# Five of eight prompt tiles gather their experts, three are multiplied with all experts in table order

## The chip, the cores and the metric

One core of one Trainium2 chip runs the whole layer as one program. The metric is device time in microseconds, the median of several runs. Everything is computed in float32.

## What is computed

One layer of an encoder over two groups of tokens, 1024 of the prompt and 256 of the sample: a mixer (windowed and dense attention, two gates, three projections), then PEER, a retrieval of experts, and an RMSNorm. The change is in PEER for the prompt:

```python
def one_chunk(xc):                      # 128 tokens of the normed input
    qry = einsum('cd,dq->cq', xc, w_query).reshape(128, 8, 2, 128)
    sc = einsum('chpd,hpnd->chpn', qry, sub_keys)         # 2 x 128 scores a head
    s_top, i_top = top_k(sc, 16)
    cand = s_top[:, :, 0, :, None] + s_top[:, :, 1, None, :]
    best_s, pos = top_k(cand.reshape(128, 8, 256), 16)
    idx = i_top[0] * 128 + i_top[1]     # taken at pos: 16 of 16384 experts a head
    g = softmax(best_s)
    u, v = expert_u[idx], expert_v[idx] # rows of 1024
    act = gelu(einsum('chkd,cd->chk', u, xc))
    return einsum('chk,chkd->cd', g * act, v)
```

A token takes 8 x 16 = 128 experts. A row of U and its row of V stand beside each other in one table `experts`, 8 KB together; the table has 16384 rows, 134 MB.

## The kernel before

The program runs its stages one after the other, with barriers between: projection, attention and merge of the sample, a stage that picks the sample's experts, then the same for the prompt with the sample's experts gathered beside them, and last `phase_experts` for the prompt's eight tiles of 128 tokens. The change replaces this last stage.

All orders are written out by hand. Each engine has its own list of instructions and waits on counters (semaphores) of the others. A tile has 128 slots (one expert for each of 128 tokens). For every slot GpSimd (POOL) issues one indirect DMA that gathers 128 rows of 8 KB into one of the RING = 8 places of `ring`, 1.05 MB (L1685). Two slots are a step, 64 steps a tile (STEPS, PAIR). In a step g, `tile` of each engine does this:

- DVE multiplies the U half of two slots with the tile's h and sums (L1930, "dot"), and multiplies the gelu of the step before with the gates (L1924, `wgt`).
- ACT takes the gelu of two dots (L1756) and writes, for the step before, two diagonal matrices from the weights (L1762, `diag`).
- PE multiplies the diagonals with the V halves and adds to `acc` in PSUM; each step is 16 products on 32x32 parts of the array, 32 records in the trace (L2032), then counts `used`.
- POOL waits for `used` of four steps back (BACK) before it gathers into the same place.

Between these steps stands the choice for the next tile, head by head: the query products (L1993), the scores (L2002), and on DVE `choose` in three parts (the top 16 of two lists of 128, then of their 256 sums, then the index: L1805 to L1859). Only head 0 of the first tile is chosen before the first gather. At the end of a tile `acc` is copied and folded (L1780, L2053), x is added (L1965), the result is normed and stored (L1971, L1662). SP's queue carries the ordinary loads: the input of a tile (`xn`), its residual (`xr`), the query weights once.

## Time and profile before

| | us |
|---|---|
| median of 3 runs | 4895.73 |
| lowest, highest | 4884.65, 4897.33 |
| profiled execution, span | 4892.3 |
| of it: stage of the prompt's experts, from its first load | 2814.8 |

Read it from the DMA side: the page gives the rate for 40 slices and splits the bytes by queue, the stretches give engines, clock and DMA share side by side, and the waits tell who is last. A line with "L" and a number is a line of the kernel before. The rows themselves stand in the section ahead of the prediction.

### The profile page before, as it was taken

The page shows a single profiled execution, that of the slowest core. Times are in us where ns is not written, and L with a number is a line of the kernel's source. Part 1 is how long each engine was busy: PE and PEld are TensorE (multiplying, and loading weights), DVE is VectorE, ACT ScalarE, POOL GpSimd, SP SyncE. Part 2 cuts the span into 40 slices and gives each one's busy share as a digit, 9 for nine tenths or more (in the row PEclk, how much of TensorE's full clock was granted, in tenths as well). Part 3 has the DMA queues.
Part 4 walks back from the last instruction along what each step waited for, and adds up shares of the span by engine and source line. Part 5 has one row for each costly group of instructions (what it writes and reads, how often), then busy time and mean ns, then how long its engine had stood idle before and what let it go on. Part 6 is the DMA issues. An engine that isn't in the chain of part 4 may idle for free.

```text
span 4892.3 us, 70239 instructions
## 1 busy us (share of the span) xinstructions
PE 3186.3 (65%) x25996; PEld 1601.2 (33%) x25996; DVE 3189.6 (65%) x7660; ACT 1006.2 (21%) x2942; POOL 1746.2 (36%) x1409
## 2 busy tenths in 40 slices
PE   8786699996999999855545445455455455454433
PEld 3444444444777744332212122122122122121000
DVE  1324756776888866568857667667667677677544
ACT  0211111222555511121121111111211211211111
POOL 0201322223443233134444444444444444444443
PEclk9988799998999999966666566556566566665555
DMA  6143598985435487599999999999999999999998
GB/s 234 62 168 138 191 342 318 359 335 193 165 147 189 153 326 300 208 379 383 390 399 393 388 390 390 393 395 386 401 394 396 399 397 394 409 392 391 408 395 330
DMA packets 281413, 1568.08 MB, mean 321 GB/s; under 512 B 27760, under 2 KB 47728, under 8 KB 112496
## 3 DMA queue, kind: packets, MB, share of 16 engines
q0 software_dynamic: 184320, 1342.26, 69.5%
q1 hardware_dynamic: 96752, 221.33, 12.2%
q8 instruction: 207, 3.39, 0.3%
q14 instruction: 134, 1.10, 0.1%
HBM read 1509.95 MB, written 53.53 MB: 320 GB/s over the span
## 4 chain that ended last, share of the span: by engine, by line
DMA 32%; issue 7%; PE 7%; DVE 5%; POOL 4%; ACT 2%; POOLq 0%; DVEq 0%; SPq 0%; ACTq 0%
DMA prompt_exp_ring<-in_experts_dram,prompt_exp_idx 29%; PE prompt_exp_acc L2032 6%; POOL prompt_exp_ring L1685 4%; DVE prompt_exp_junk L1930 3%; DMA prompt_exp_ring<-in_experts_dram,prompt_exp_idx_all 3%; ACT prompt_exp_diag L1762 2%; PE prompt_exp_qp L1993 1%; DVE prompt_exp_pos L1809 0%; DVE prompt_exp_best L1805 0%; DVE prompt_exp_dot L1930 0%; DMA prompt_exp_wq<-in_w_query_dram 0%; DVE prompt_exp_crest L1814 0%; DVE prompt_exp_hit L1852 0%; DVE prompt_exp_hit L1846 0%; DVE prompt_exp_cand L1829 0%
## 5 line engine op out<-in xcount | busy, mean ns | idle before, releaser
L2032 PE MATMUL prompt_exp_acc<-prompt_exp_ring,prompt_exp_diag 32*32 32x512 f32 x16384 | 938.9, 945 | 1407.8 <-ACT prompt_exp_diag L1762 1407.2
L1930 DVE CUSTOM_DVE_ANT_0 prompt_exp_junk<-prompt_exp_ring,prompt_exp_h_now 128x1024 bf16<-128x1024 f32 x1024 | 1246.1, 1228 | 711.6 <-DMA prompt_exp_ring<-in_experts_dram,prompt_exp_idx 667.0
L1685 POOL DMA_INDIRECT prompt_exp_ring<-in_experts_dram,prompt_exp_idx x896 | 1036.3, 1157 | 1368.8 <-PE prompt_exp_acc L2032 1202.3
L2032 PEld LDWEIGHTS prompt_exp_acc<-prompt_exp_ring,prompt_exp_diag 32*32 32x32 f32 x16384 | 169.3, 127 | 1959.5 <-issue 1957.3
L151 POOL DMA_INDIRECT sample_hid_ring<-in_experts_dram,sample_hid_idx x256 | 278.1, 1087 | 891.9 <-DVE sample_hid_acc L181 842.7
L1756 ACT ACTIVATE prompt_exp_ge<-prompt_exp_dot 128x2 f32<-128x2 f32 x512 | 104.1, 203 | 2297.5 <-DVE prompt_exp_dot L1930 2297.4
L536 PE MATMUL prompt_proj_acc<-normed_w,normed_hT 128*128 128x512 f32 x1280 | 553.8, 595 | 14.5 <-PEq L90 14.5
L164 DVE CUSTOM_DVE_ANT_0 sample_hid_junk<-sample_hid_ring,sample_hid_h 128x1024 bf16<-128x1024 f32 x256 | 349.6, 1366 | 41.7 <-DMA sample_hid_ring<-in_experts_dram,sample_hid_idx 31.7
L1993 PEld LDWEIGHTS prompt_exp_qp<-prompt_exp_hT,prompt_exp_wq 128*128 128x128 f32 x2048 | 312.2, 242 | 143.6 <-issue 140.9
L536 PEld LDWEIGHTS prompt_proj_acc<-normed_w,normed_hT 128*128 128x128 f32 x1280 | 243.6, 191 | 318.5 <-issue 318.5
L1993 PE MATMUL prompt_exp_qp<-prompt_exp_hT,prompt_exp_wq 128*128 128x128 f32 x2048 | 335.5, 332 | 2.3 <-DMA prompt_exp_wq<-in_w_query_dram 2.3
L181 DVE SCALAR_TENSOR_TENSOR sample_hid_acc<-sample_hid_ring,sample_hid_w,sample_hid_acc 128x1024 f32<-128x1024 f32 x254 | 326.2, 1284 | 7.4
L1762 ACT ACTIVATE prompt_exp_diag<-prompt_exp_fold,prompt_exp_wgt 128x32 f32<-128x32 f32 x1024 | 264.5, 306 | 0.6 <-issue 0.2
L1685 POOL DMA_INDIRECT prompt_exp_ring<-in_experts_dram,prompt_exp_idx_all x128 | 150.4, 1175 | 263.9 <-PE prompt_exp_acc L2032 147.7
L536 PE MATMUL sample_proj_acc<-sample_proj_w,sample_proj_hT 128*128 128x512 f32 x320 | 140.9, 603 | 9.4 <-PEq L270 9.4
L1924 DVE TENSOR_TENSOR prompt_exp_wgt<-prompt_exp_ge,prompt_exp_g_now 128x2 f32<-128x2 f32 x512 | 83.3, 163 | 97.7 <-ACT prompt_exp_ge L1756 90.0
L173 DVE TENSOR_TENSOR sample_hid_w<-sample_hid_ge,sample_hid_g 128x1 f32<-128x1 f32 (+1 forms) x208 | 61.3, 295 | 114.7 <-ACT sample_hid_ge L202 114.4
L997 PE MATMUL prompt_att_Op<-prompt_att_vB,prompt_att_pT_b 128*128 128x128 f32 x1024 | 125.9, 276 | 10.4 <-ACT prompt_att_pT_a L711 10.4
L997 PEld LDWEIGHTS prompt_att_Op<-prompt_att_vB,prompt_att_pT_b 128*128 128x128 f32 x1024 | 119.3, 192 | 13.6 <-ACT prompt_att_pT_a L711 13.6
L967 PE MATMUL prompt_att_Sb<-prompt_att_kTB,prompt_att_qT 128*128 128x512 f32 x256 | 121.7, 598 | 0.0
L1211 PE MATMUL prompt_mrg_Y<-prompt_mrg_wb,prompt_mrg_mixT 128*128 128x512 f32 x256 | 112.5, 592 | 0.0
L1234 PE MATMUL prompt_mrg_Z<-prompt_mrg_wo,prompt_mrg_mT 128*128 128x512 f32 x256 | 111.3, 593 | 1.1 <-ACT prompt_mrg_mT L1160 1.1
(318 smaller groups left out, 4035.2 us busy)
## 6 DMA issues: line engine op xcount, KB each, us to landing
sample_proj_w<-in_w_all_dram SPq DMA_DIRECT2D x10, 2048.0 KB, 13.6
normed_w<-in_w_all_dram SPq DMA_DIRECT2D x10, 2048.0 KB, 18.0
proj_dram<-prompt_proj_stage SPq DMA_DIRECT2D x80, 256.0 KB, 6.0
prompt_exp_ring<-in_experts_dram,prompt_exp_idx POOLq DMA_INDIRECT x896, 8.7
sample_qry_wq<-in_w_query_dram SPq DMA_DIRECT2D x4, 2048.0 KB, 10.2
prompt_att_q<-proj_dram SPq DMA_DIRECT2D x16, 512.0 KB, 4.8
mixed_dram<-prompt_att_OT SPq DMA_DIRECT2D x8, 1024.0 KB, 3.8
prompt_mrg_mixT<-mixed_dram SPq DMA_DIRECT2D x8, 1024.0 KB, 10.7
```

The lines of the kernel that those rows point to most:

```text
L151: self.nc.gpsimd.indirect_dma_start(out=self.ring[:, s % self.RING, :], out_offset=None, in_=self.experts, in_offset=bass.IndirectOffsetOn ...
L164: self.nc.vector.tensor_tensor_reduce(out=self.junk[:], in0=self.ring[:, s % self.RING, 0:D], in1=self.h[:], scale=1.0, scalar=0.0, op0=AL ...
L181: nc.vector.scalar_tensor_tensor(self.acc[:], v, w, self.acc[:], ALU.mult, ALU.add).then_inc(self.added, 1)
L536: last = nc.tensor.matmul(acc[:, u % 4, :], hT[:, k, t * P:(t + 1) * P], w[:, c % NL, k, :], start=(k == 0), stop=(k == KD - 1))
L967: last = nc.tensor.matmul(Sb[:, c:c + w], qT[:, i % 2, 8 + g, :], kTB[:, g // 4, c:c + w], start=True, stop=True)
L997: last = nc.tensor.matmul(Op[:, 1, g % 4 * BD:g % 4 * BD + BD], pT_b[:, t * P:(t + 1) * P], vB[:, t, g // 4 * BD:g // 4 * BD + BD], start= ...
L1211: last = nc.tensor.matmul(Y[:, br, h * 512:h * 512 + 512], mixT[:, i % 2, (br * KD + k) * P:(br * KD + k + 1) * P], w[h][:, k, :], start=( ...
L1685: nc.gpsimd.indirect_dma_start(out=ring[:, s % RING, :], out_offset=None, in_=experts, in_offset=bass.IndirectOffsetOnAxis(ap=column(s), a ...
L1762: last = nc.scalar.activation(diag[:, (g - 1) % 2, c, :], fold[:], ACT.Copy, scale=wgt[:, s:s + 1])
L1930: nc.vector.tensor_tensor_reduce(out=junk[:, s % 2, :], in0=ring[:, s % RING, 0:D], in1=h_now[:], scale=1.0, scalar=0.0, op0=ALU.mult, op1 ...
L1993: last = nc.tensor.matmul(qp[:, h % 2, p * P:(p + 1) * P], wq[:, k, (2 * h + p) * P:(2 * h + p + 1) * P], hT[:, k * P:(k + 1) * P], start= ...
L2032: last = nc.tensor.matmul(acc[at:at + Q, rows, :], diag[k, (g - 1) % 2, c, :], ring[k, s % RING, D + half * 512:D + half * 512 + 512], sta ...
```

## The change

`phase_mixed` takes the place of `phase_experts` for the prompt. Tiles 0 to 4 are gathered as before, with the same steps. Tiles 5 to 7, 384 tokens, are multiplied with all 16384 experts; a gate matrix, zero for the experts that a token has not chosen, makes the sum the same. One class, `Turns`, walks through the whole stage and calls each engine's part in the same order:

1. Eight tiles are normed and turned. The h of tiles 1 to 4 goes to DRAM.
2. 32 query units of eight products of 512 columns (four tiles at once) and their scores. The scores go to DRAM (`scores_dram`, stored by ACT in `spread_s`) and are loaded again for each head's choice. The heads of tiles 0, 5 and 6 are chosen here; from unit 9 on two steps follow each unit.
3. The gate matrices, 96 blocks of 4 tokens: for each token DVE writes a one-hot matrix of 128 slots by 128 first indices, scaled with the gate (`build_a`), ACT one of the second indices by an Abs and a Relu (`build_b`), PE multiplies them to 128x128, ACT copies the product from PSUM in another order (`spread_b`) and after every 8 blocks stores 2 MB to `gates_dram` in pieces of 512 bytes. 40 steps are interleaved, and tile 7's heads.
4. 32 chunks of 4 x 128 experts: four units of `stage1` (eight products of 384 columns with a turned copy of U, 512 KB a unit), gelu on ACT, one product with the gates on DVE (`mult`), six units of `stage2` (four products of 512 columns with V), each added on DVE to a sum in SBUF (`add`). 229 steps are spread evenly by the cost 5.2 and 3.5 of a unit. `finish` adds, norms and stores the three tiles.

`Turns.advance` counts a tile as 65 entries: 64 steps with rows and one that only uses up the last pair. A turned copy of U is a further input, prepared on the host.

In the order of PE, before, in the middle of a tile (qp is the query product, acc the gathered sum):

```order
L2032 MATMUL prompt_exp_acc<-prompt_exp_ring,prompt_exp_diag 32x512 x16
L1993 MATMUL prompt_exp_qp<-prompt_exp_hT,prompt_exp_wq 128x128 x8
L2032 MATMUL prompt_exp_acc<-prompt_exp_ring,prompt_exp_diag 32x512 x48
L2002 MATMUL prompt_exp_sc<-prompt_exp_keys,prompt_exp_qT 128x128 x2
L2032 MATMUL prompt_exp_acc<-prompt_exp_ring,prompt_exp_diag 32x512 x32
```

and in the change, in the dense part (L2281 is stage 1, L2297 stage 2, L2261 a step):

```order
L2281 MATMUL prompt_exp_wk<-prompt_exp_hT,prompt_exp_area 128x384 x8
L2261 MATMUL prompt_exp_acc<-prompt_exp_ring,prompt_exp_diag 32x512 x16
L2281 MATMUL prompt_exp_wk<-prompt_exp_hT,prompt_exp_area 128x384 x8
L2261 MATMUL prompt_exp_acc<-prompt_exp_ring,prompt_exp_diag 32x512 x16
L2297 MATMUL prompt_exp_wk<-prompt_exp_area 128x512 x8
L2261 MATMUL prompt_exp_acc<-prompt_exp_ring,prompt_exp_diag 32x512 x16
L2281 MATMUL prompt_exp_wk<-prompt_exp_hT,prompt_exp_area 128x384 x8
L2261 MATMUL prompt_exp_acc<-prompt_exp_ring,prompt_exp_diag 32x512 x16
```

Steps that stood alone or beside a query product of 128 columns now stand each behind eight products of 384 or 512 columns.

In the order of ACT, before, there is nothing but the steps (L1756, L1762) and a copy:

```order
L1756 ACTIVATE prompt_exp_ge<-prompt_exp_dot 128x2
L1762 ACTIVATE prompt_exp_diag<-prompt_exp_fold,prompt_exp_wgt 128x32 x2
L1718 COPY prompt_exp_qT<-prompt_exp_qp 128x256
L1756 ACTIVATE prompt_exp_ge<-prompt_exp_dot 128x2
L1762 ACTIVATE prompt_exp_diag<-prompt_exp_fold,prompt_exp_wgt 128x32 x2
```

and in the change, while the gates are built (L1946 Abs, L1948 Relu, L1955 the copy from PSUM, L1959 the store):

```order
L1946 ACTIVATE prompt_exp_area<-prompt_exp_iota,prompt_exp_ijgT 128x128 x4
L1948 ACTIVATE prompt_exp_area<-prompt_exp_area 128x512
L1955 COPY prompt_exp_area<-prompt_exp_wk 128x128x4
L1959 DMA gates_dram<-prompt_exp_area 128x32x128
L1966 ACTIVATE prompt_exp_ge<-prompt_exp_dot 128x2
L1973 ACTIVATE prompt_exp_diag<-prompt_exp_fold,prompt_exp_wgt 128x32 x2
L1946 ACTIVATE prompt_exp_area<-prompt_exp_iota,prompt_exp_ijgT 128x128 x4
```

A step of ACT now stands behind two or three blocks, and after every eighth behind a store of 4096 pieces.

The diff, cut to its core:

```diff
-def phase_experts(nc, sems, tag, nt, x2, g_ffn, w_query, sub_keys, experts, g_final, ident_d, iota_d, fold_d, unfold_d, out, kept=None):
...
+GATHERED, DENSE = (0, 1, 2, 3, 4), (5, 6, 7)
+NORM_ORDER = (0, 5, 6, 7, 1, 2, 3, 4)
+TURNED = len(DENSE) * P
+JB = 4
+EXPERT_CHUNKS = KEYS // JB
+PAIR = 2
+STEPS = SLOTS // PAIR
+BLOCK = 4
+BLOCKS = P // BLOCK
...
+    def advance(self, k, whole=True):
+        for _ in range(k):
+            if self.e == len(GATHERED) * (STEPS + 1):
+                return
+            n, g = divmod(self.e, STEPS + 1)
+            self.e += 1
+            self.on("step", n, g)
+            if g == STEPS:
+                self.on("close", n)
+                continue
+            octet, off = 8 * n + g // 8, g % 8
+            head = octet + 4
+            if not 8 <= head < HEADS * len(GATHERED):
+                continue
+            tile, h = divmod(head, HEADS)
+            if whole and off == 1:
+                for part in range(3):
+                    self.on("choose", tile, h, part)
+            if not whole and off in (1, 3, 5):
+                self.on("choose", tile, h, off // 2)
+            if h % 4 == 3 and off == 6:
+                self.on("soften", tile, slice(h - 3, h + 1))
+            if h % 4 == 3 and off == 7:
+                self.on("gates", tile, slice(h - 3, h + 1))
+    def pick(self, tile, h):
+        for part in range(3):
+            self.on("choose", tile, h, part)
+    def walk(self):
+        on, first, every = self.on, DENSE[0], slice(0, HEADS)
+        for v in range(37):
+            if v < 32:
+                on("query", v)
+            if 1 <= v <= 32:
+                on("spread_q", v - 1)
+            if v % 2 and 3 <= v <= 33:
+                on("scores", (v - 3) // 2)
+            if v % 2 == 0 and 4 <= v <= 34:
+                on("spread_s", (v - 4) // 2)
+            if v >= 5 and v % 4 == 1 and v < 37:
+                h = (v - 5) // 4
+                if h < HEADS:
+                    self.pick(GATHERED[0], h)
+                    on("soften", GATHERED[0], slice(h, h + 1))
+            if v >= 6 and v % 4 == 2 and (v - 6) // 4 < HEADS:
+                self.pick(first, (v - 6) // 4)
+            if v >= 8 and v % 4 == 0 and (v - 8) // 4 < HEADS:
+                self.pick(first + 1, (v - 8) // 4)
+            if v >= 7 and v % 4 == 3 and (v - 7) // 4 < HEADS:
+                on("gates", GATHERED[0], slice((v - 7) // 4, (v - 7) // 4 + 1))
+            if v == 34:
+                on("soften", first, every)
+            if v == 35:
+                on("gates", first, every)
+                on("turn", 0)
+            if v >= 9:
+                self.advance(2)
+        on("soften", first + 1, every)
+        done = 0
+        def blocks(k):
+            nonlocal done
+            for _ in range(k):
+                on("block", done)
+                if done:
+                    on("spread_b", done - 1)
+                done += 1
+        for k in range(HEADS):
+            self.pick(first + 2, k)
+            if k == 1:
+                on("gates", first + 1, every)
+                on("turn", 1)
+            blocks(3)
+            self.advance(1)
+            blocks(3)
+            self.advance(1)
+        on("soften", first + 2, every)
+        for k in range(12):
+            blocks(2)
+            self.advance(1)
+            if k == 1:
+                on("gates", first + 2, every)
+                on("turn", 2)
+            blocks(2)
+            self.advance(1)
+        on("spread_b", done - 1)
+        on("built")
+        assert done == len(DENSE) * BLOCKS
+        before, rest = self.e, len(GATHERED) * (STEPS + 1) - self.e
+        cost = {"1": 5.2, "2": 3.5}
+        whole = EXPERT_CHUNKS * (4 * cost["1"] + 6 * cost["2"])
+        spent, last = 0.0, None
+        def settle():
+            if last and last[0] == "1":
+                on("gelu", last[1])
+            elif last:
+                on("add", *last[1:])
+        for c in range(EXPERT_CHUNKS + 1):
+            for kind, u in (("1", 0), ("1", 1), ("2", 0), ("2", 1), ("1", 2), ("2", 2), ("2", 3), ("1", 3), ("2", 4), ("2", 5)):
+                if c == (EXPERT_CHUNKS if kind == "1" else 0):
+                    continue
+                unit = ("1", JB * c + u) if kind == "1" else ("2", c - 1, u)
+                on("stage1" if kind == "1" else "stage2", *unit[1:])
+                settle()
+                last = unit
+                spent += cost[kind]
+                self.advance(before + round(rest * min(1.0, spent / whole)) - self.e, False)
+            if c == 0 or c == EXPERT_CHUNKS:
+                settle()
+                last = None
+            if c < EXPERT_CHUNKS:
+                on("mult", c)
+        on("finish")
+        self.advance(rest, False)
...
+                def load_scores(i):
...
+                    at = NORM_ORDER.index(tile)
+                    b, x = 2 * h + at // 4, at % 4 // 2
+                    sp.wait_ge(s_stored[x], 16 * (b + 1))
+                    if i >= 2:
+                        sp.wait_ge(scl_free, i - 1)
...
+                def load_u(j):
+                    if j < 3:
+                        sp.wait_ge(s_full, 32)
+                    else:
+                        sp.wait_ge(s1_full, j - 2)
+                    sp.dma_start(ut[:, j % 3, :, :], u_turned[j].rearrange("p (k c) -> p k c", k=KD)).then_inc(u_ld[j % 3], 16)
+                def load_v(c, half):
+                    src = experts.rearrange("(i j) c -> i j c", j=KEYS)
+                    at = D + half * 512
+                    sp.dma_start(vt[:, half, :, :], src[:, c * JB:(c + 1) * JB, at:at + 512]).then_inc(v_ld[half], 16)
+                def load_gates(c):
+                    sp.dma_start(gc[:, c % 2, :, :, :].rearrange("p k j t -> p k (j t)"),
+                                 gates_d[c].rearrange("k p f -> p k f")).then_inc(gc_ld[c % 2], 16)
...
+                def spread_s(b):
+                    h, grp = divmod(b, 2)
+                    for x in range(2):
+                        act.wait_ge(s_full, 2 * b + x + 1)
+                        if b:
+                            act.wait_ge(s_stored[x], 16 * b)
+                        nc.scalar.copy(scs[:, x, :], wk[:, 2 + x, :]).then_inc(s_ready, 1)
+                        act.wait_ge(s_ready, 2 * b + x + 1)
+                        at = 4 * grp + 2 * x
+                        act.dma_start(scores_d[h, at:at + 2].rearrange("y p f -> p y f"),
+                                      scs[:, x, :].rearrange("p (y f) -> p y f", y=2)).then_inc(s_stored[x], 16)
...
+                def build_b(i):
...
+                    for c in range(BLOCK):
+                        t = BLOCK * k + c
+                        last = nc.scalar.activation(apart[:, c, :], iota[:], ACT.Abs, bias=ijgT[:, d % 2, 1, t:t + 1], scale=-1.0)
+                    link(last)
+                    nc.scalar.activation(onehot_b[:, i % 2, :, :], apart, ACT.Relu, bias=1.0, scale=-1.0).then_inc(b_ready, 1)
+                def spread_b(i):
+                    k, t = divmod(i, Q // BLOCK)
+                    act.wait_ge(gp_full, i + 1)
+                    if t == 0 and k >= 2:
+                        act.wait_ge(built_stored[k % 2], 16 * (k // 2))
+                    nc.scalar.copy(built[:, k % 2, :, :, BLOCK * t:BLOCK * t + BLOCK].rearrange("p c j t -> p (c j) t"),
+                                   wk[:, 2 + i % 2, :].rearrange("p (t j) -> p j t", t=BLOCK)).then_inc(gp_spread, 1)
+                    if t == Q // BLOCK - 1:
+                        act.wait_ge(gp_spread, i + 1)
+                        act.dma_start(gates_d.rearrange("c k p f -> p c k f")[:, :, k, :],
+                                      built[:, k % 2, :, :, :].rearrange("p c j t -> p c (j t)")).then_inc(built_stored[k % 2], 16)
...
+                def gelu(j):
...
+                    nc.scalar.activation(act_e[:, c % 2, j % JB, :], wk[:, j % 2, 0:TURNED], ACT.Gelu).then_inc(ge_ready, 1)
...
+                def build_a(i):
...
+                    for c in range(BLOCK):
+                        t = BLOCK * k + c
+                        last = nc.vector.tensor_scalar(onehot_a[:, i % 2 * BLOCK + c, :], iota[:], ijgT[:, d % 2, 0, t:t + 1],
+                                                       ijgT[:, d % 2, 2, t:t + 1], ALU.is_equal, ALU.mult)
+                    last.then_inc(a_ready, 1)
...
+                def mult(c):
+                    dve.wait_ge(ge_ready, JB * (c + 1))
+                    dve.wait_ge(gc_ld[c % 2], 16 * (c // 2 + 1))
+                    e = act_e[:, c % 2, :, :].rearrange("p j (k t) -> p j k t", t=Q)
+                    nc.vector.tensor_tensor(e, e, gc[:, c % 2, :, :, :].rearrange("p k j t -> p j k t"), ALU.mult).then_inc(multed, 1)
+                def add(c, g):
+                    half, t = divmod(g, ND)
+                    o, to = 6 * c + g, oacc[:, t, half * 512:half * 512 + 512]
+                    dve.wait_ge(s2_full, o + 1)
+                    if c == 0:
+                        nc.vector.tensor_copy(to, wk[:, 2 + o % 2, :]).then_inc(added, 1)
+                    else:
+                        dve.wait_ge(added, o - 5)
...
+                def stage1(j):
+                    pe.wait_ge(u_ld[j % 3], 16 * (j // 3 + 1))
+                    if j < 2:
+                        pe.wait_ge(ij_spread, ND)
+                    else:
+                        pe.wait_ge(ge_ready, j - 1)
+                    for k in range(KD):
+                        last = nc.tensor.matmul(wk[:, j % 2, 0:TURNED], ut[:, j % 3, k, :], hT_dense[:, k, :],
+                                                start=(k == 0), stop=(k == KD - 1))
+                def stage2(c, g):
...
+                        last = nc.tensor.matmul(wk[:, 2 + o % 2, :], act_e[:, c % 2, j, t * P:(t + 1) * P], vt[:, half, j, :],
+                                                start=(j == 0), stop=(j == JB - 1))
...
-        phase_experts(nc, sems, f"{tag}_exp{t0}", G, x2_[rows, :], g_ffn, w_query, sub_keys, experts, g_final, ident, iota,
...
+        phase_mixed(nc, tag + "_exp", x2_, g_ffn, w_query, sub_keys, experts, u_turned, g_final, ident, iota, fold, unfold,
+                    scratch("scores_dram", (HEADS, PT_, P, 2 * KEYS)), scratch("h_dram", (len(GATHERED) - 1, P, D)),
+                    scratch("gates_dram", (EXPERT_CHUNKS, TURNED // Q, P, JB * Q)), out_)
...
+        "u_turned": np.asarray(expert_u)[0].reshape(KEYS, KEYS, KD, P).transpose(1, 3, 2, 0).reshape(KEYS, P, D),
```

## Rows read from the trace of the kernel before

**Rows 1.** The cores view: span and mean granted clock.

```profile
core 0: 4892.3 us, clock 0.751
```

**Rows 2.** The page: GB/s in 40 slices; the software queue.

```profile
GB/s 234 62 168 138 191 342 318 359 335 193 165 147 189 153 326 300 208 379 383 390 399 393 388 390 390 393 395 386 401 394 396 399 397 394 409 392 391 408 395 330
...
q0 software_dynamic: 184320, 1342.26, 69.5%
```

**Rows 3.** Stretches: us, busy by engine (PE, PEld, DVE, ACT, POOL), clock, DMA, GB/s.

```profile
1100.00:1400.00 300.00, 244.94 (x1507) 177.77 (x1506) 233.53 (x466) 137.82 (x292) 123.27 (x75) 0.93 0.45 170
1400.00:1700.00 300.00, 283.79 (x1956) 220.49 (x1954) 261.27 (x571) 175.96 (x375) 102.41 (x68) 1.00 0.44 163
...
3480.00:3830.00 350.00, 175.78 (x2392) 71.20 (x2392) 239.28 (x619) 54.23 (x219) 153.69 (x132) 0.61 0.99 396
...
4530.00:4870.00 340.00, 135.33 (x2084) 24.28 (x2096) 173.34 (x327) 46.06 (x198) 143.23 (x126) 0.51 1.00 400
```

**Rows 4.** Waits from 2400 to 4800 us: total, times, longest.

```profile
PE prompt_exp_acc L2032 <- ACT prompt_exp_diag L1762: 1221.0, 423, 7.0
POOL prompt_exp_ring L1685 <- PE prompt_exp_acc L2032: 1191.0, 427, 6.7
DVE prompt_exp_junk L1930 <- DMA prompt_exp_ring<-in_experts_dram,prompt_exp_idx: 634.7, 539, 3.0
```

**Rows 5.** SP's timeline: start us, us; residual loads.

```profile
2477.43 0.32 SPq L1656 DMA_DIRECT2D prompt_exp_xr<-x_dram  x1
...
4545.62 0.32 SPq L1656 DMA_DIRECT2D prompt_exp_xr<-x_dram  x1
```

**Rows 6.** Timeline of the stage's start, all engines.

```profile
2077.49 0.32 SPq L1626 DMA_DIRECT2D prompt_exp_xn<-x_dram  x1
...
2086.71 1.01 ACT L1714 COPY prompt_exp_hT<-prompt_exp_qp 128x1024 f32<-128x1024 f32 x1 [4.18 <-PE prompt_exp_qp L1984]
...
2096.90 0.50 DVE L1805 MAX8 prompt_exp_top<-prompt_exp_sc 128x8 f32<-128x128 f32 x2 [12.31 <-PE prompt_exp_sc L2002]
...
2106.74 0.17 DVE L1870 TENSOR_TENSOR prompt_exp_soft<-prompt_exp_best 128x16 f32<-128x16 f32 x1
...
2107.50 0.94 POOL L1685 DMA_INDIRECT prompt_exp_ring<-in_experts_dram,prompt_exp_idx_all  x1 [66.04 <-DVEq L1867]
```

**Rows 7.** Timeline of the end: the last diag.

```profile
4873.26 0.94 ACT L1762 ACTIVATE prompt_exp_diag<-prompt_exp_fold,prompt_exp_wgt 128x32 f32<-128x32 f32 x4
```

**Rows 8.** PE: a group of the page; two steps in the timeline.

```profile
L536 PE MATMUL prompt_proj_acc<-normed_w,normed_hT 128*128 128x512 f32 x1280 | 553.8, 595 | 14.5 <-PEq L90 14.5
...
3201.95 2.19 PE L2032 MATMUL prompt_exp_acc<-prompt_exp_ring,prompt_exp_diag 32*32 32x512 f32 x32 [6.37 <-ACT prompt_exp_diag L1762]
...
3207.67 1.14 PE L2032 MATMUL prompt_exp_acc<-prompt_exp_ring,prompt_exp_diag 32*32 32x512 f32 x32
```

**Rows 9.** Groups of the page; one weight product in the timeline.

```profile
L1930 DVE CUSTOM_DVE_ANT_0 prompt_exp_junk<-prompt_exp_ring,prompt_exp_h_now 128x1024 bf16<-128x1024 f32 x1024 | 1246.1, 1228 | 711.6 <-DMA prompt_exp_ring<-in_experts_dram,prompt_exp_idx 667.0
...
L1756 ACT ACTIVATE prompt_exp_ge<-prompt_exp_dot 128x2 f32<-128x2 f32 x512 | 104.1, 203 | 2297.5 <-DVE prompt_exp_dot L1930 2297.4
...
L1762 ACT ACTIVATE prompt_exp_diag<-prompt_exp_fold,prompt_exp_wgt 128x32 f32<-128x32 f32 x1024 | 264.5, 306 | 0.6 <-issue 0.2
...
3201.41 0.16 DVE L1924 TENSOR_TENSOR prompt_exp_wgt<-prompt_exp_ge,prompt_exp_g_now 128x2 f32<-128x2 f32 x1 [0.27 <-ACT prompt_exp_ge L1756]
```

**Rows 10.** Groups by shape, 0 to 2078 us.

```profile
L472 ACT COPY prompt_proj_kT<-prompt_proj_tpA 128x512 f32<-128x512 f32 x8 | 4.5, 569 | 0.0
...
L864 DVE TENSOR_TENSOR prompt_att_O<-prompt_att_Op,prompt_att_rinv 128x512 f32<-128x512 f32 x32 | 22.1, 691 | 1.1
```

**Rows 11.** SP's timeline: loads of 1024 pieces each.

```profile
51.89 0.43 SPq L357 DMA_DIRECT2D sample_proj_w<-in_w_all_dram  x1
...
1150.19 1.18 SPq L732 DMA_DIRECT2D prompt_att_vA<-proj_dram  x1
1151.43 8.96 SPq L733 DMA_DIRECT2D prompt_att_vB<-proj_dram  x1
```

894 lines of the change are left out of this document (455 added, 439 removed).

## The prediction

> **What bounds the kernel now.** First the cores view: one core, span 4892.3 us, mean granted clock 0.751 [rows 1]. Then the page's slices and DMA table: from the eighteenth slice on the transfer rate stands near 390 to 400 GB/s, and nearly all of it is the software queue, which is the gather [rows 2]. The stage of the prompt's experts runs from its first load at 2077.49 to the end of the span: 2815 us, 58% of the kernel. There I read the stretches: DMA share 0.99 to 1.00 at 396 to 400 GB/s, PE busy for 40 to 50% of the time, at a granted clock of 0.51 to 0.61 [rows 3]. The waits in such a stretch say the same: PE waits for ACT's diag, POOL waits for PE, and the chain ends at DVE waiting for gathered rows, 635 us [rows 4]. The residual load of tile 1 and that of tile 7 are issued 2068.2 us apart [rows 5]: 344.7 us for a tile, 2.69 us for a slot of 1.05 MB, 5.39 us for a step of two slots. All eight tiles' 1024 slots cost 8 x 344.7 = 2758 us, the first gather is issued 30.0 us after the stage's start [rows 6], and some 20 us of closing follow the last diag [rows 7]. These make up the 2815 us. The gather's bytes bound the stage, with a ring of four steps just deep enough to keep the queues full.
>
> **What the change does to the bytes.** Five tiles still gather: 640 slots, 671 MB. Three tiles read every expert once: U turned 67 MB, V 67 MB. Gates go out and come back, 25 MB each way, scores 8.4 MB each way. Together 872 MB instead of 1074 MB, or 2208 us instead of 2719 us at 395 GB/s. If DMA stayed full, the change would win some 500 us. The question is how much of that is lost where DMA can't be full, and whether PE, which now has to multiply 384 tokens with 16384 experts, holds the pace. I cut the new stage where `walk` cuts it.
>
> **Entry, up to the first step: 118 us, added over the old 30 us.** Before, the one tile's turned copy was there 10.2 us after its load was issued [rows 6]. Now eight tiles are normed and turned before the first query, two of them in flight, so the other seven cost between nothing but ACT's own work and the whole 10.2 us each; I take half of it, since two buffers alternate: 10 + 7 x 5 = 45 us. Then nine query units. A 128x512 f32 product takes two records of 0.433 us each [rows 8], so 0.865 us, eight of them 6.9 us; nine units 62 us, and 11 us for scores that now go to DRAM and back.
>
> **Queries with two steps each (28 units): 402 us.** DVE is last here. Choosing a head costs 9.8 us, from the first MAX8 to the next operation behind it [rows 6]; a step costs two dots of 1.23 us, the weights 0.16 us and a wait of 0.27 us for ACT's gelu, 2.9 us [rows 9]. A unit with a head: 9.8 + 5.8 = 15.6 us; three of four have one, the fourth takes 6.5 us. Seven rounds of 53.3 us, and three heads ahead of their tile (29 us). PE needs 6.9 + 2 x 1.14 us + about 1 us of scores = 10 us a unit at full clock and 20 us at half; the same step of 32 records takes 1.14 us at one clock and 2.19 us at the other [rows 8]. In stretches where PE was busy for 82% and 95% the clock was 0.93 and 1.00 [rows 3]; for 70% here I take about 0.8, where DVE is still the later one. The score's way through DRAM lies beside DVE's previous pick of 15 us and costs nothing as long as store and load stay under that.
>
> **Building the gates (96 blocks, 40 steps): 467 us.** ACT is last. A block: four Abs of 128x128 at 0.32 us (on the line between a diag of 128x32, 264.5 / 1024 = 0.258 us [rows 9], and a copy of 128x512, 0.57 us [rows 10]), one Relu and one PSUM copy of 128x512 at 0.57 us each, and 0.4 us of hand-overs: 2.8 us. Six blocks, two steps (0.2 + 0.52 us each on ACT [rows 9]) and 6.3 us in which ACT waits for DVE's head: 24.6 us, eight times, 197 us. Then four blocks and two steps 12.7 us, twelve times, 152 us. Two or three heads ahead 25 us, three turns 9 us. The twelve stores of 2 MB in pieces of 512 bytes are issued by ACT itself. No DMA was issued by ACT before; SP's issues bound this one: a load of 1024 pieces with an empty queue took 0.43 us, the second of two such loads 8.96 us [rows 11]. A store here has 4096 pieces. Between 0.4 and 20 us I take 7 us, nearer to the 8.96 us row: 84 us. DVE's 345 us of work and PE's products lie under ACT.
>
> **Dense multiplication with 229 steps: 1740 us.** PE: stage 1 is 128 x 8 products of 384 columns, 0.649 us each at full clock, 665 us; stage 2 is 768 products of 512 columns, 664 us; 225 steps at 1.14 us, 257 us; closings 14 us: 1600 us at full clock. DMA: 225 steps of 2.1 MB, 472 MB, with U, V, gates and small loads 642 MB: 1625 us at 395 GB/s. DVE has 1090 us (450 dots 558, weights and waits 97, 24 heads 234, 192 additions at 0.69 us 132 [rows 10], gate products about 56), ACT about 230 us; both are covered. The two large ones are nearly equal and are coupled in order: a step stands in PE's queue behind a product of up to 5.2 us, so a ring slot comes free up to 5.2 us later, while POOL's pieces of the loop stay. PE's clock at 90% busy lies between the two stretches above, about 0.97, which makes PE 1650 us. To the larger of both I add 5% for waits on either side: 1740 us, 7.6 us a step. The bounds are 1640 us (nothing lost) and 1970 us (the loop of four slots at 8.6 us a step).
>
> **Sum.** 118 + 402 + 467 + 1740 + 20 (closing as before, since the dense tiles finish beside the last steps) = 2747 us against 2815 us: 68 us less, a span of 4824 us. The median of the runs lies 3.4 us over the profiled span; I predict **4830 us**.
>
> **The rivals.**
> (1) *The floor.* DMA never starves in the dense part, 1640 us: 4730 us. For it: 1.00 DMA share with a ring of the same depth before. Against: PE had half of its time free then.
> (2) *ACT's stores hold it.* Each store of 4096 pieces keeps ACT in its issue until most pieces have gone, beside gathers: 25 us each, 216 us more, 5045 us. From 12.7 us a store on, the whole gain is gone. For it: the 8.96 us row with 1024 pieces. This is the rival on the other side.
> (3) *The loop.* A step waits for the product ahead of it in PE's queue and the product for the step: 8.6 us a step, 1970 us, 5060 us. It decides from 7.9 us a step on.
> (4) *The clock.* In the gather stretches the clock stood at 0.51 to 0.61 with PE 40 to 50% busy [rows 3]. Should the dense part stand at 0.8, PE needs 2000 us: 5090 us. Against: it is 90% busy.
> (5) *V's rows.* One V load reads 128 partitions whose rows lie 1 MB apart; the gather's rows are random, and its 395 GB/s need not hold for that. If V's bytes take twice their time, DMA rises by 170 us, of which PE's slack covers little: about 5000 us. The page "DMA: Bandwidth & Descriptors" of the Trainium skill (Latency and other measured facts) says that copies with a row pitch of 512 KiB fell to 207 GB/s and with 2 MiB to 164 GB/s; by that V's loads would cost about what this rival says. No run here has such a pitch yet.
>
> **How the numbers follow.** The forecast has 0.42 (0.34 of it faster by over 0.3%, 0.06 within, 0.02 slower), the floor 0.13, ACT's stores 0.12, the loop 0.16, the clock 0.06, V's rows 0.11. The last four hold 0.45, of which 0.02 end faster and 0.03 within 0.3%, when only a part of their price comes true. That gives faster 0.49, same 0.09, slower 0.42, where 0.3% is about what a measurement can tell from no change. The range from 4700 to 5060 us leaves out under 0.1 on each side; the forecast's own range is 4760 to 4910 us.
>
> **What the new profile would show.** Right: the first gather some 95 us after the stage's start; DVE over 90% busy in the query part while DMA is at 60%; in the dense part DMA share above 0.93 and PE above 0.9 busy, clock above 0.95, a step every 7.6 us. Wrong in size: an ACT queue row for the gates' store of over 12 us; PE's longest waits on U or V loads (V's rows) or on diag (the loop); GB/s under 360 at a DMA share of 1.0 in the dense part; a clock under 0.9 there. If the part before the dense one takes more than 1055 us, or the dense one more than 1808 us, with the other as forecast, the change doesn't pay.

## The result and the profile after

The changed kernel takes **4690.51 us** (median of four runs, 4685.90 to 4700.05) against 4892.60 us for the kernel before (four runs, 4884.65 to 4897.33): ratio 0.9581, 95% interval 0.9558 to 0.9604. The forecast was 4830 us with a range from 4700 to 5060 us. The sign was right; the gain is 202 us where I forecast 66 us, and the time lies 10 us under the range.

The cores view, and from the page the slices of TensorE (PE), its clock and the transfers, and the software queue:

```profile
core 0: 4689.9 us, clock 0.926
```

```profile
PE   8786599996999989968875446499999999999998
...
PEclk9888799998999999988887667799999999999999
DMA  6243398886444467754888669999999999999997
GB/s 236 72 176 122 141 369 313 348 340 237 179 165 171 154 248 309 285 215 151 338 319 323 228 221 352 350 361 389 372 406 386 389 380 400 397 381 382 403 385 293
...
q0 software_dynamic: 129024, 939.58, 50.8%
```

Before, the clock was 0.751 over the span [rows 1] and the gather filled the transfers near 390 GB/s from the eighteenth slice on [rows 2]. Now the stage has a front part at 151 to 352 GB/s (nineteenth to twenty-sixth slice) and a long back part in which PE is at 9 tenths and the clock at full speed. The software queue moved 1342 MB before and 940 MB now.

The same stretches as in my forecast, now cut at the first gate product and at the first product of stage 1 (columns: stretch, us, busy by PE, PEld, DVE, ACT, POOL, clock, DMA share, GB/s):

```profile
2075.00:2619.00 544.00, 375.01 (x2595) 164.57 (x2595) 387.36 (x1301) 116.70 (x300) 122.15 (x118) 0.79 0.74 284
2619.00:2996.00 377.00, 201.70 (x2039) 137.84 (x2040) 298.62 (x1005) 254.26 (x698) 85.16 (x76) 0.73 0.76 279
2996.00:4674.00 1678.00, 1620.66 (x10864) 717.82 (x10864) 934.28 (x2226) 236.16 (x846) 493.22 (x446) 0.99 0.98 382
```

The last row is the one to read against [rows 3]. There the transfers stood at 0.99 to 1.00 with PE busy for 40 to 50% at a clock of 0.51 to 0.61. Here PE is busy for 1621 of 1678 us (97%) at 0.99 of its clock, and the transfers are still at 0.98. One row can't say which of the two sets the time. The waits of the dense part (total, times, longest) and the groups and the chain of the page point to PE:

```profile
POOL prompt_exp_ring L1882 <- PE prompt_exp_acc L2261: 1073.9, 218, 34.7
DVE prompt_exp_area L2167 <- PE prompt_exp_wk L2297: 583.3, 143, 15.7
PE prompt_exp_wk L2281 <- DMA prompt_exp_area<-in_u_turned_dram: 29.4, 1, 29.4
DVE prompt_exp_junk L2132 <- DMA prompt_exp_ring<-in_experts_dram,prompt_exp_idx: 21.7, 23, 3.7
PE prompt_exp_acc L2261 <- ACT prompt_exp_diag L1973: 20.3, 46, 1.3
```

```profile
L2281 PE MATMUL prompt_exp_wk<-prompt_exp_hT,prompt_exp_area 128*128 128x384 f32 x2048 | 691.6, 491 | 29.4 <-DMA prompt_exp_area<-in_u_turned_dram 29.4
L2297 PE MATMUL prompt_exp_wk<-prompt_exp_area 128*128 128x512 f32 x1536 | 698.6, 602 | 0.0
...
L2261 PE MATMUL prompt_exp_acc<-prompt_exp_ring,prompt_exp_diag 32*32 32x512 f32 x10240 | 399.7, 654 | 172.7 <-ACT prompt_exp_diag L1973 168.0
```

Before, DVE waited 635 us for gathered rows and PE 1221 us for the diag, in 2400 us [rows 4]; now these are 22 and 20 us in 1640 us of the dense part, and DVE and POOL wait for PE. Stage 1 (L2281) and stage 2 (L2297) never wait for a transfer except once, 29.4 us at the start of the part.

### The profile page after: what moved, and what is told of

Read it like the earlier page. It is cut to its first block, busy times and chain, and to the rows that moved or that the text cites. A ratio compares the mean times of both kernels' runs of the same rounds, so it can differ in the third digit from the quotient of the medians.

```text
span 4689.9 us, 61734 instructions
## 1 busy us (share of the span) xinstructions
PE 4012.9 (86%) x22629; PEld 2067.2 (44%) x22629; DVE 2925.1 (62%) x7301; ACT 1187.7 (25%) x3085; POOL 1256.7 (27%) x1018
## 3 DMA queue, kind: packets, MB, share of 16 engines
q1 hardware_dynamic: 208976, 393.37, 23.1%
## 4 chain that ended last, share of the span: by engine, by line
PE 34%; DVE 12%; DMA 5%; issue 3%; ACT 2%; POOL 0%; SPq 0%; DVEq 0%; ACTq 0%
PE prompt_exp_wk L2281 13%; PE prompt_exp_wk L2297 11%; PE prompt_exp_acc L2261 6%; DVE prompt_exp_junk L2132 4%; PE prompt_exp_wk L2211 2%; DMA prompt_exp_ring<-in_experts_dram,prompt_exp_idx 2%; DMA gates_dram<-prompt_exp_area 1%; PE prompt_exp_wk L2246 1%; DVE prompt_exp_topi L2038 1%; DVE prompt_exp_top L2035 1%; DVE prompt_exp_hT L2116 1%; DVE prompt_exp_pos L2038 1%; DVE prompt_exp_best L2035 1%; DMA prompt_exp_ysq<-x_dram 1%; ACT prompt_exp_diag L1973 1%
## 5 line engine op out<-in xcount | busy, mean ns | idle before, releaser
L1882 POOL DMA_INDIRECT prompt_exp_ring<-in_experts_dram,prompt_exp_idx x640 | 700.5, 1095 | 1907.6 <-PE prompt_exp_acc L2261 1666.7
L2132 DVE CUSTOM_DVE_ANT_0 prompt_exp_junk<-prompt_exp_ring,prompt_exp_h 128x1024 bf16<-128x1024 f32 x640 | 762.1, 1222 | 79.1 <-DMA prompt_exp_ring<-in_experts_dram,prompt_exp_idx 78.6
L2281 PE MATMUL prompt_exp_wk<-prompt_exp_hT,prompt_exp_area 128*128 128x384 f32 x2048 | 691.6, 491 | 29.4 <-DMA prompt_exp_area<-in_u_turned_dram 29.4
L2297 PE MATMUL prompt_exp_wk<-prompt_exp_area 128*128 128x512 f32 x1536 | 698.6, 602 | 0.0
L2261 PE MATMUL prompt_exp_acc<-prompt_exp_ring,prompt_exp_diag 32*32 32x512 f32 x10240 | 399.7, 654 | 172.7 <-ACT prompt_exp_diag L1973 168.0
L2281 PEld LDWEIGHTS prompt_exp_wk<-prompt_exp_hT,prompt_exp_area 128*128 128x128 f32 x2048 | 382.5, 190 | 360.3 <-issue 92.2
L2167 DVE TENSOR_TENSOR prompt_exp_area<-prompt_exp_area,prompt_exp_wk 128x512 f32<-128x512 f32 x186 | 127.8, 687 | 627.2 <-PE prompt_exp_wk L2297 585.9
L2297 PEld LDWEIGHTS prompt_exp_wk<-prompt_exp_area 128*128 128x128 f32 x1536 | 280.9, 190 | 415.8 <-issue 381.3
L2246 PE MATMUL prompt_exp_wk<-prompt_exp_area,prompt_exp_hT 128*128 128x128 f32 x768 | 143.6, 349 | 137.1 <-DVE prompt_exp_hT L2116 95.4
L2261 PEld LDWEIGHTS prompt_exp_acc<-prompt_exp_ring,prompt_exp_diag 32*32 32x32 f32 x10240 | 79.5, 107 | 375.9 <-ACT prompt_exp_diag L1973 259.7
L2246 PEld LDWEIGHTS prompt_exp_wk<-prompt_exp_area,prompt_exp_hT 128*128 128x128 f32 x768 | 126.2, 251 | 191.1 <-DVE prompt_exp_hT L2116 129.6
L997 PE MATMUL prompt_att_Op<-prompt_att_vB,prompt_att_pT_b 128*128 128x128 f32 x1024 | 125.9, 276 | 10.4 <-ACT prompt_att_pT_a L711 10.4
```

Of the source, the lines that this page charges most:

```text
L1882: nc.gpsimd.indirect_dma_start(out=ring[:, s % RING, :], out_offset=None, in_=experts, in_offset=bass.IndirectOffsetOnAxis(ap=idx[:, n % 2 ...
L2132: nc.vector.tensor_tensor_reduce(out=junk[:, s % 2, :], in0=ring[:, s % RING, 0:D], in1=h2[:, n % 2, :], scale=1.0, scalar=0.0, op0=ALU.mu ...
L2246: last = nc.tensor.matmul(wk[:, 2 + i % 2, c * KEYS:(c + 1) * KEYS], onehot_a[:, i % 2 * BLOCK + c, :], onehot_b[:, i % 2, c, :], start=Tr ...
L2261: last = nc.tensor.matmul(acc[at:at + Q, part, :], diag[k, (g - 1) % 2, c, :], ring[k, s % RING, D + half * 512:D + half * 512 + 512], sta ...
L2281: last = nc.tensor.matmul(wk[:, j % 2, 0:TURNED], ut[:, j % 3, k, :], hT_dense[:, k, :], start=(k == 0), stop=(k == KD - 1))
L2297: last = nc.tensor.matmul(wk[:, 2 + o % 2, :], act_e[:, c % 2, j, t * P:(t + 1) * P], vt[:, half, j, :], start=(j == 0), stop=(j == JB - 1))
```

## The experiments

In all of them the time is compared with the kernel before on the same chip; the changed kernel's own ratio is 0.9581.

### Which of the two bounds the dense part: less work for PE

```diff
-                        last = nc.tensor.matmul(wk[:, j % 2, 0:TURNED], ut[:, j % 3, k, :], hT_dense[:, k, :],
+                        last = nc.tensor.matmul(wk[:, j % 2, 0:2 * P], ut[:, j % 3, k, :], hT_dense[:, k, 0:2 * P],
```

> The dense stage 1 multiplies 256 of the 384 columns (one of the three dense tiles is left out of it, so its output is not the reference's); all transfers stay. TensorE loses 128 x 8 products x 128 columns, a third of the 690 us of that line, 225 us; the bytes stay. TensorE is the bound (its wait is what the ring's loads wait for, 1074 us, and it is busy 98% of the dense part): the dense part falls from 1678 us until the transfers are the bound at 395 to 400 GB/s, 1605 to 1625 us, so the kernel is 50 to 75 us faster, 4615 to 4640 us. Transfers are the bound (their share is 0.99): no change, 4690 us within 10 us.

Measured: 4696.94 us, ratio 0.9587 (0.9569 to 0.9605): no gain from a tenth less of PE's work. The dense stretch of this kernel, the group of stage 1 with what it waited for over the whole run, and two of its rows in PE's timeline:

```profile
3000.00:4680.00 1680.00, 1448.49 (x10878) 744.91 (x10864) 936.58 (x2225) 232.29 (x845) 504.19 (x446) 0.94 0.98 381
```

```profile
L2281 PE MATMUL prompt_exp_wk<-prompt_exp_hT,prompt_exp_area x2048: 379/379/796, 3000.1 to 4644.0; 128*128 128x256 f32 x187
its engine sat idle before it (us, times) until:
  DMA prompt_exp_area<-in_u_turned_dram: 316.8, 33
```

```profile
3606.75 6.30 PE L2281 MATMUL prompt_exp_wk<-prompt_exp_hT,prompt_exp_area 128*128 128x256 f32 x16 [10.38 <-DMA prompt_exp_area<-in_u_turned_dram]
...
3622.29 3.62 PE L2281 MATMUL prompt_exp_wk<-prompt_exp_hT,prompt_exp_area 128*128 128x256 f32 x16
```

PE's busy time fell by 172 us and all of it came back as waits, for the U loads above all, with DMA at 0.98. A wait costs twice: the same 16 records take 6.30 us behind a wait of 10.4 us and 3.62 us in a busy stretch. The granted clock shows it; these are the 7 us in which they ran behind the wait and the 9 us after them (the clock is the third number from the end):

```profile
3606.00:3613.00 7.00, 6.25 (x19) 4.80 (x19) 0.00 (x0) 0.00 (x0) 0.00 (x0) 0.57 0.58 223
3613.00:3622.00 9.00, 9.00 (x81) 3.46 (x81) 2.35 (x2) 1.00 (x4) 4.32 (x4) 1.00 0.82 281
```

Over the dense part the mean clock is 0.94 instead of 0.99. Taken alone this run says "the transfers bound it".

### The other side: fewer bytes

```diff
-                    sp.dma_start(ut[:, j % 3, :, :], u_turned[j].rearrange("p (k c) -> p k c", k=KD)).then_inc(u_ld[j % 3], 16)
+                    sp.dma_start(ut[:, j % 3, 0:KD // 2, :], u_turned[j].rearrange("p (k c) -> p k c", k=KD)[:, 0:KD // 2, :]
+                                 ).then_inc(u_ld[j % 3], 16)
...
-                    sp.dma_start(vt[:, half, :, :], src[:, c * JB:(c + 1) * JB, at:at + 512]).then_inc(v_ld[half], 16)
+                    sp.dma_start(vt[:, half, 0:JB // 2, :], src[:, c * JB:c * JB + JB // 2, at:at + 512]).then_inc(v_ld[half], 16)
```

> Half of every load of U and of V is left out in the dense part (the products then read older contents, so the outputs of the dense tiles are not the reference's); all products stay. 67 MB of 642 MB go, TensorE's work stays. TensorE is the bound: within 15 us of 4690 us, some of it from the start of the part. Transfers are the bound: 67 MB at 390 GB/s are 170 us, so about 4520 us.

Measured: 4689.56 us, ratio 0.9581 (0.9565 to 0.9597), the same again. Its dense stretch:

```profile
2996.00:4671.00 1675.00, 1621.33 (x10864) 718.39 (x10862) 931.58 (x2226) 235.46 (x843) 491.51 (x446) 0.99 0.91 343
```

A tenth of the bytes is gone, the rate fell from 382 to 343 GB/s, PE's busy time and the time are what they were. Taken alone this run says "PE bounds it". Either both stand so close that lightening one shows the other, or something third holds both.

### Both at once, against the loop of the ring

The two edits above in one kernel.

> Both edits of the two earlier runs at once: stage 1 without the third dense tile's columns, and half of each load of U and V left out (the dense tiles' outputs are not the reference's). Each alone left the time where it was. Theory of two bounds that stand abreast: TensorE's busy time in the dense part is 1612 - 174 = 1440 us, the bytes are 575 MB, 1482 us at 388 GB/s, so the part falls from 1680 to about 1500 us and the kernel to about 4510 us. Rival, the loop of four steps (a third thing that neither edit touches: POOL waits for the release of a ring place, and the place comes back after load, dot, gelu, diag and product): the time stays at 4690 us within 15 us.

Measured: 4549.89 us, ratio 0.9290 (0.9268 to 0.9311): 141 us less than the changed kernel. Its dense stretch:

```profile
2990.00:4530.00 1540.00, 1421.03 (x10858) 727.91 (x10856) 934.24 (x2224) 231.03 (x842) 508.59 (x445) 0.98 0.96 373
```

The two bounds are real, and they stand abreast: only with both lightened does a step go down, from 7.3 to 6.7 us. Nothing that neither edit touches holds the part. That alone doesn't rule out the loop of four steps, rival (3), since the loop runs through the product ahead of a step in PE's queue, and the thin stage 1 shortens that product from 5.32 to 3.62 us too. What speaks against the loop is PE's own waits in the changed kernel: a loop that came last would leave PE waiting for the diag between its products, and it waited for it 20 us in all. The size I expected, 180 us, was too large: 1540 us is 8% over PE's 1421 us. Where neither has slack, the coupling that I had put at 5% does show; the changed kernel, with PE at 97%, doesn't pay it.

### V from a contiguous copy

```diff
-                    src = experts.rearrange("(i j) c -> i j c", j=KEYS)
-                    at = D + half * 512
-                    sp.dma_start(vt[:, half, :, :], src[:, c * JB:(c + 1) * JB, at:at + 512]).then_inc(v_ld[half], 16)
+                    sp.dma_start(vt[:, half, :, :], v_turned[c, half].rearrange("p (j x) -> p j x", j=JB)).then_inc(v_ld[half], 16)
...
+        "v_turned": np.asarray(expert_v)[0].reshape(KEYS, EXPERT_CHUNKS, JB, 2, 512).transpose(1, 3, 0, 2, 4
+                                                     ).reshape(EXPERT_CHUNKS, 2, P, JB * 512),
```

> V is read from a copy laid out beforehand so that one load of 1 MB is one contiguous stretch, in place of 128 partitions whose rows lie 1 MB apart; same bytes, same products. V's rows cost next to nothing (TensorE is the bound, and the rate was 380 to 402 GB/s with them): within 10 us of 4690 us. V's rows take twice their time, as my rival had it, but TensorE hides it: also no change in time, but the transfer share of the dense part falls by about 0.05 or more. V's rows cost and transfers are the bound: up to 170 us faster, 4520 us.

Measured: 4693.91 us, ratio 0.9590 (0.9574 to 0.9606): nothing. But this was asked where PE hides the answer, so it was asked again on top of the thin stage 1, where the transfers come last:

> Stage 1 without the third dense tile's columns (its output is not the reference's), so that TensorE has slack and waits for the U loads, and V read from a contiguous copy. With TensorE as second bound out of the way, V's rows have to show if they cost transfer time: if they take twice their time, up to 170 us less than the thin kernel's 4697 us, 4530 to 4600 us; if they cost what the other bytes cost, 4697 us within 12 us.

Measured: 4645.64 us, ratio 0.9482 (0.9460 to 0.9504), 51 us less than the thin kernel:

```profile
2999.00:4631.00 1632.00, 1440.18 (x10878) 737.73 (x10864) 937.97 (x2225) 231.47 (x845) 500.16 (x446) 0.96 0.99 393
```

At nearly the same DMA share (0.99 and 0.98) the rate is 393 instead of 381 GB/s. How much of the 51 us is the time of V's transfers themselves is read from the queue of the ordinary loads (packets, MB, time of its packets as a share of 16 engines' span): of the thin kernel, of the thin kernel with the flat V, of the changed kernel, and of the changed kernel with the flat V.

```profile
q1 hardware_dynamic: 208976, 393.37, 23.0%
```

```profile
q1 hardware_dynamic: 184400, 393.37, 22.8%
```

```profile
q1 hardware_dynamic: 208976, 393.37, 23.1%
```

```profile
q1 hardware_dynamic: 184400, 393.37, 22.7%
```

With the spans, 4696.8, 4647.5, 4689.9 and 4682.1 us, these are 1080, 1060, 1083 and 1063 us. So the flat V takes some 20 us from the packets' time in both pairs (to within about 5 us, since the shares are rounded). In the second pair the kernel's time doesn't follow: there PE hides it. At 395 GB/s V's 67 MB would take 170 us; as they lie in the table they take about an eighth more, not the twice of rival (5). The rest of the 51 us lies in PE: in the dense stretch it stood idle for 192 instead of 232 us, at a clock of 0.96 instead of 0.94, and no run takes apart why. The flat copy makes the pieces longer too (184400 packets instead of 208976, for the same bytes), and these runs don't separate the pitch of 1 MB from the piece of 2 KB.

The Trainium skill ("DMA: Bandwidth & Descriptors", Latency and other measured facts) gives for copies 207 GB/s at a pitch of 512 KiB and 164 GB/s at 2 MiB, and calls 214 GB/s the full rate of such a copy. An estimate from these figures is 1.03 to 1.3 times the full-rate time for V's pitch of 1 MB, which lies between. The trace agrees: about 1.1. My prediction had held the 207 and 164 GB/s against the 395 GB/s of the gathers here, and so had read half speed out of them.

### The gate stores

The rows of ACT's twelve stores in the changed kernel, and what they made wait:

```profile
L1959 ACTq DMA_DIRECT2D gates_dram<-prompt_exp_area x12: 366/366/370, 2659.5 to 2996.8; - x12
its engine sat idle before it (us, times) until:
who waited for it (us, times):
  ACT prompt_exp_area L1955: 10.9, 2
```

0.37 us each, where I had 7 us each, 84 us together. To see whether that is a price of the store or of its place, each was issued twice:

```diff
-                        act.dma_start(gates_d.rearrange("c k p f -> p c k f")[:, :, k, :],
-                                      built[:, k % 2, :, :, :].rearrange("p c j t -> p c (j t)")).then_inc(built_stored[k % 2], 16)
+                        for to in (gates_d, gates2_d):
+                            act.dma_start(to.rearrange("c k p f -> p c k f")[:, :, k, :],
+                                          built[:, k % 2, :, :, :].rearrange("p c j t -> p c (j t)")).then_inc(built_stored[k % 2], 16)
```

> Each of the twelve gate stores that ScalarE issues is issued a second time, into a second scratch tensor; 25 MB more are written. A store costs ScalarE 0.37 us (its queue rows): 12 x 0.37 = 4 us, and 25 MB more of writing beside a transfer share of 0.8: the building part 377 us grows by 4 to 40 us, the kernel by 10 to 50 us, of which most would be the last store's landing before the first gate load. A store costs ScalarE the 7 us of my forecast, hidden in waits that other rows carry: at least 84 us, 4775 us or more.

Measured: 4770.93 us, ratio 0.9750 (0.9733 to 0.9766): 80 us more. ACT's timeline at one pair, and the building as a stretch, whole and its front part alone:

```profile
2804.75 12.65 ACTq L1962 DMA_DIRECT2D gates_dram<-prompt_exp_area  x2
```

```profile
2613.00:3064.00 451.00, 203.77 (x2039) 138.07 (x2040) 297.36 (x1005) 254.24 (x700) 86.20 (x76) 0.70 0.83 285
```

```profile
2613.00:2850.00 237.00, 103.61 (x891) 72.70 (x891) 168.61 (x599) 129.72 (x341) 28.96 (x30) 0.67 0.72 240
```

A pair holds ACT for 5.7 to 14.9 us, the twelve together for 125 us. The building went from 377 to 451 us with nearly the same busy time on every engine. In the front part the transfers aren't full (share 0.72), so the added bytes can't be the price there: six pairs held ACT for 55 us, and the seventh was issued 31 us later in the building than the seventh store of the changed kernel. My expectation for the cheap store was wrong too: the price isn't one of the store, it is one of a store behind another. The next run puts the second store half a turn of eight blocks later:

```diff
                         act.dma_start(gates_d.rearrange("c k p f -> p c k f")[:, :, k, :],
                                       built[:, k % 2, :, :, :].rearrange("p c j t -> p c (j t)")).then_inc(built_stored[k % 2], 16)
+                    if t == 3 and k >= 1:
+                        act.dma_start(gates2_d.rearrange("c k p f -> p c k f")[:, :, k - 1, :],
+                                      built[:, (k - 1) % 2, :, :, :].rearrange("p c j t -> p c (j t)")
+                                      ).then_inc(built_stored[(k - 1) % 2], 16)
```

> Eleven of the twelve gate stores are issued a second time into a scratch tensor as in the run with doubled stores (+80 us, 6 to 14 us in the queue for a pair), but half a turn of eight blocks after the first, when that one has had 12 us or more to go. The issue waits for room behind the store before it: then the spaced ones cost far less than the pairs, 11 x 0.4 us and the bytes beside a transfer share of 0.8: 4700 to 4725 us. The 23 MB themselves cost the time (6.7 us a store of 2.1 MB is close to its bytes at 310 GB/s): again about 4765 us.

Measured: 4728.75 us, ratio 0.9658 (0.9637 to 0.9678): 38 us more, half way, just outside what I expected. The timeline of ACT and two stretches:

```profile
2836.16 0.37 ACTq L1964 DMA_DIRECT2D gates_dram<-prompt_exp_area  x1
...
2870.11 8.84 ACTq L1964 DMA_DIRECT2D gates_dram<-prompt_exp_area  x1
...
...
2900.10 15.70 ACTq L1964 DMA_DIRECT2D gates_dram<-prompt_exp_area  x1
```

```profile
2617.00:2850.00 233.00, 114.32 (x1030) 79.45 (x1029) 186.52 (x662) 144.02 (x381) 36.43 (x36) 0.70 0.79 271
2850.00:3030.00 180.00, 86.31 (x993) 55.74 (x1008) 111.64 (x344) 109.17 (x317) 50.71 (x39) 0.73 1.02 362
```

Up to 2850 us, at a DMA share of 0.79, six extra stores, 10 to 22 us behind the store before, cost 0.37 to 0.72 us each and the same work took 233 us (231 us in the changed kernel). Behind 2850 us, where the gathers fill the transfers, a store isn't through in the 10 to 12 us until the next one, which then holds ACT for 8.8 to 15.7 us: five holds, 67 us, and 180 us in place of 146. One store there, 22 us behind the one before, took 2.03 us. The bytes themselves cost nothing as long as the share is 0.79. Behind 2850 us, at 1.02, this run can't say: 362 GB/s over 180 us are 12.6 MB more than the changed kernel's 360 GB/s over 146 us, and 12.6 MB at that rate are 35 us, as much as the part grew. The changed kernel issues its stores 22 to 39 us apart, and each took 0.37 us, also at its share of 0.96 behind 2850 us.

### How many steps lie in the building

Sixty instead of forty (the second of each pair of steps doubled in both loops), and twenty (the first of each pair left out):

```diff
             blocks(3)
             self.advance(1)
             blocks(3)
-            self.advance(1)
+            self.advance(2)
...
             blocks(2)
-            self.advance(1)
+            self.advance(2)
         on("spread_b", done - 1)
```

> 60 gather steps instead of 40 lie in the gate building, 205 instead of 225 in the dense part. TensorE bounds the dense part: it loses 20 x 1.14 = 23 us there; the building part has no full engine (DVE 77%, ScalarE 62%, transfers 0.78) but its order makes each step wait, so it grows by 20 x (about 3 us of ScalarE and DVE) = 60 us: 4690 + 37 = about 4727 us. Transfers bound the dense part: it loses 20 x 2.1 MB at 390 GB/s = 108 us, the building grows by 60 us: about 4640 us.

Measured: 4739.82 us, ratio 0.9696 (0.9671 to 0.9722).

```diff
             blocks(3)
-            self.advance(1)
+            self.advance(0)
...
             blocks(2)
-            self.advance(1)
+            self.advance(0)
             if k == 1:
```

> 20 gather steps instead of 40 in the gate building, 245 instead of 225 in the dense part. With 60 the building grew by 72 us (3.6 us a step) and the dense part fell by 35 us. Two bounds abreast: the building falls by 72 us, and the dense part, bound by transfers on this side, grows by 20 x 2.1 MB at 390 GB/s = 108 us: about 4725 us. TensorE alone the bound: it grows by 20 x 1.14 = 23 us, so about 4640 us.

Measured: 4727.60 us, ratio 0.9654 (0.9635 to 0.9674). The dense part behind its start, with 60 steps, in the changed kernel (40), and with 20:

```profile
3500.00:4500.00 1000.00, 984.58 (x6318) 442.08 (x6317) 554.88 (x1338) 138.90 (x487) 279.70 (x254) 1.00 0.97 372
```

```profile
3500.00:4500.00 1000.00, 982.59 (x6594) 435.60 (x6592) 583.71 (x1413) 144.35 (x515) 303.73 (x274) 1.00 1.00 390
```

```profile
3500.00:4500.00 1000.00, 950.77 (x6559) 416.03 (x6558) 593.20 (x1450) 146.31 (x517) 310.21 (x281) 0.98 1.00 391
```

From the first records of the products: with 60 steps the building takes 462 us (85 more) and the dense part 1643 us (35 less); with 20 it takes 336 us (41 less) and the dense part 1760 us (82 more). On one side PE is at 98% and the transfers have room, on the other the transfers are at 1.00 and PE waits; the changed kernel has PE at 98% and the transfers at 1.00. The 60 steps came out near what PE alone tells (4727 us), since PE is the later one on that side; the building took 85 us for them where I had 60 us, and the dense part gave back 35 us where I had 23 us. Both directions lose 37 to 49 us, so the split in the changed kernel lies near its best. The run with 20 steps stands with the two bounds abreast (4725 us) and not with PE alone (4640 us), but that it lies within 3 us is luck: the building gave 41 us where I expected 72 us (the 72 us for the 60 steps in that expectation were too low as well, they took 85 us), and the dense part took 82 us where I expected 108 us. Even with the 41 us, PE alone would give about 4672 us.

### The wait at the start of the dense part

SP's timeline there (start us, us) and PE's row:

```profile
3029.70 1.15 SPq L1812 DMA_DIRECT2D prompt_exp_area<-gates_dram  x2
3030.91 3.61 SPq L1809 DMA_DIRECT2D prompt_exp_area<-in_experts_dram  x2
3034.56 1.77 SPq L1804 DMA_DIRECT2D prompt_exp_area<-in_u_turned_dram  x3
```

```profile
3044.60 6.81 PE L2281 MATMUL prompt_exp_wk<-prompt_exp_hT,prompt_exp_area 128*128 128x384 f32 x16 [29.41 <-DMA prompt_exp_area<-in_u_turned_dram]
```

SP stands 33 us in the wait for the last gate store (issued at 2996.8), and the fourth U load is queued behind. The first edit moves SP's wait behind the fourth and fifth U load:

```diff
                     if j + 3 < KEYS:
                         load_u(j + 3)
+                    if j == 1:
+                        gates_and_v()
...
-                walk(query=query, spread_s=spread_s, choose=choose, step=step, built=all_built, stage1=stage1, stage2=stage2,
+                walk(query=query, spread_s=spread_s, choose=choose, step=step, stage1=stage1, stage2=stage2,
```

> SP waits for the gates' last store only behind the U loads of stage 1's third and fourth products groups, so that TensorE doesn't stand 29.4 us before the fourth one; nothing else changes. TensorE is the bound of the dense part: 20 to 29 us faster, 4661 to 4671 us. Transfers are the bound: the rate stood at 386 GB/s before that wait and 324 to 327 GB/s in the 70 us from it on, so only some 10 us of bytes were lost there: 4680 us.

Measured: 4682.65 us, ratio 0.9576 (0.9552 to 0.9600), 8 us less by the medians and not separable from the changed kernel. PE still waits; its wait, and SP's timeline:

```profile
PE prompt_exp_wk L2283 <- DMA prompt_exp_area<-in_u_turned_dram: 23.9, 1, 23.9
```

```profile
2996.40 6.76 SPq L1804 DMA_DIRECT2D prompt_exp_area<-in_u_turned_dram  x2
3030.80 1.15 SPq L1812 DMA_DIRECT2D prompt_exp_area<-gates_dram  x2
...
3035.87 0.86 SPq L1804 DMA_DIRECT2D prompt_exp_area<-in_u_turned_dram  x1
```

The two loads that the edit moved came in time: PE now multiplied five groups before it waited, where it had multiplied three. But the sixth U load still stood behind SP's wait and was issued at 3035.87, and PE waited for that one. So the edit moved the wait by two groups and didn't take it away. Together with the 60 steps (both diffs above) it changed nothing that can be measured:

> Both edits: U loads ahead of the wait for the gates, and 60 steps in the building. The sum of both results, by either theory: TensorE the bound 4690 + 37 - 25 = about 4702 us, transfers the bound 4690 - 50 - 10 = about 4630 us.

Measured: 4737.63 us, ratio 0.9689 (0.9665 to 0.9713).

### A version that takes from PE's side

Four products groups of stage 1 go into the last third of the building, the next four stand ahead of the first gate multiplication, and SP's wait for the gates comes behind their U loads.

```diff
         for k in range(12):
+            if k % 2 == 0 and k >= 4:
+                on("stage1", k // 2 - 2)
             blocks(2)
+            if k % 2 == 0 and k >= 4:
+                on("gelu", k // 2 - 2)
...
-        for c in range(EXPERT_CHUNKS + 1):
-            for kind, u in (("1", 0), ("1", 1), ("2", 0), ("2", 1), ("1", 2), ("2", 2), ("2", 3), ("1", 3), ("2", 4), ("2", 5)):
-                if c == (EXPERT_CHUNKS if kind == "1" else 0):
+        mixed = (("1", 0), ("1", 1), ("2", 0), ("2", 1), ("1", 2), ("2", 2), ("2", 3), ("1", 3), ("2", 4), ("2", 5))
+        for c in range(1, EXPERT_CHUNKS + 1):
+            for kind, u in (sorted(mixed) if c == 1 else mixed):
+                if c == 1 and (kind, u) == ("2", 0):
+                    settle()
+                    last = None
+                    on("mult", 0)
+                if c == EXPERT_CHUNKS and kind == "1":
```

> The same order of the products without the flat V. Two bounds abreast: TensorE gets its 50 us, the transfers stay the bound of the dense part, where the kernel with the thin stage 1 showed 1680 us; only what the transfers lost at the part's start (some 10 us) is to be had: 4675 to 4695 us. TensorE alone the bound: 4645 us, the same as with the flat V.

Measured: **4672.31 us**, ratio 0.9540 (0.9520 to 0.9560), the fastest whole kernel of this study. And with the flat V on top:

> Nothing is left out. V is read from the contiguous copy, and the four stage 1 products groups of the first dense chunk run in the last third of the gate building, where TensorE is half idle, with the second chunk's four ahead of the first gate multiplication, so that the wait for the last gate store and the 24 to 29 us wait for U are bridged. Two bounds abreast: TensorE's side of the dense part falls by 21 us of products and up to 29 us of wait, the transfers' side by the 51 us that the flat V gave the thin kernel, the building grows by a few us: 4640 to 4660 us. Should the building pay for the four groups in full (21 us, since its order makes every hand-over wait): 4665 us. Rival, one bound that neither edit touches: 4690 us.

Measured: 4672.73 us, ratio 0.9547 (0.9525 to 0.9569): the flat V adds nothing, against what I expected. The dense stretch of the first of the two, and from the second what DVE waits for at its start:

```profile
2998.00:4651.00 1653.00, 1599.88 (x10816) 705.64 (x10800) 935.56 (x2226) 233.95 (x838) 494.96 (x446) 0.99 0.99 386
```

```profile
DVE prompt_exp_area L2166 <- DMA prompt_exp_area<-gates_dram: 23.5, 1, 23.5
```

21 us of PE's products left the dense part, which is 25 us shorter (1653 us); the building ends 2 us later. The medians show 18 us gained, and the intervals of the two kernels just overlap. The bridge failed: the wait for U became a wait for the gates, 24.5 us at PE against 29.4 us, since the last store has to land first (40 us behind its issue here, 33 us in the changed kernel) and the four groups and their steps last only some 25 us. And the transfers, at 386 GB/s, didn't stop this kernel where they stopped the thin one, at 381 GB/s and 4697 us. So the transfers are no hard floor at one figure. Between 3500 and 4500 us they moved 390 GB/s in the changed kernel and 393 GB/s here, with PE at 98% in both, but 384 GB/s in the thin one; where they come last, PE's waits for U and its lower clock behind them add to it. How much of that is the clock and how much the order of U loads among the gathers, no run here tells apart.

## Why the prediction was wrong, point by point

**What bounds the kernel and the bytes: right.** The dense part moved 382 GB/s x 1678 us = 641 MB, forecast 642 MB. PE and the transfers were forecast within 2% of each other (1650 and 1625 us), and three runs show that neither has more than a few per cent of slack: one side lighter, the other side lighter, both.

**Entry and queries: right within 5%.** The first gather is issued 90.8 us after the stage's start (forecast 95). Entry and queries took 544 us (forecast 520), DVE busy for 81% between 2190 and 2600 us where I said over 90%. DVE waited twice for scores on their way back from DRAM, which I had called free:

```profile
DVE prompt_exp_top L2035 <- DMA prompt_exp_scl<-scores_dram: 20.9, 2, 15.4
```

That is about the 24 us by which the part is longer; no run took this wait away, so it is only argued.

**Building the gates: the failed step, 80 of the 90 us.** The part took 377 us, forecast 467. Without the stores my sum was 383 us, and that holds. The term "twelve stores at 7 us" measured 12 x 0.37 us, with 10.9 us of waits for them. I had the right rows [rows 11]: 0.43 us for a load alone and 8.96 us for the second of two. The error was to take the second row as the nearer one because a store has more pieces. The stores stand 22 to 39 us apart, so each of them is "the first". The runs with doubled stores show both prices: 0.37 us where the one before is through, 6 to 16 us where it isn't. Rival (2) was this same mechanism. Even with the stores in pairs it would not have reached its size: a pair held ACT for 10.4 us in the mean, not 25 us, and that kernel was still 122 us faster than the one before.

**The dense part: the second failed step, 62 us.** 1678 us, forecast 1740. PE's busy time is 1621 us where I had 1600 us (groups 692 and 699 us instead of 665 and 664), at a clock of 0.99 to 1.00 where I took 0.97. The 5% for "waits on either side" (83 us) came out as 57 us, of which 29 us is the one wait at the start. So of the 62 us, 29 us are PE's time (1621 instead of 1650 us, since the clock was higher than I took), 26 us are the coupling, and 7 us are a slip in the sum: 1650 us and 5% are 1733 us, not 1740 us. I had added it to the larger of two bounds as if both had to be late now and then. With PE last and the ring four steps deep, PE hardly waited for the transfers behind the start: 982.6 us of 1000 us busy. The coupling exists: in the kernel with both sides lighter the part was 8% over PE's busy time.

**Closing:** 16 us, forecast 20.

**The rivals.** The floor (1) was nearest in its time (4730 us) but not in its reason: its dense part of 1640 us with 7 us stores was 1678 us with free ones, and its 1640 us lay below my own 1650 us for PE. The loop (3), 8.6 us a step, didn't come: a step took 7.3 us and PE hardly waited for the diag. The clock (4) went the other way. V's rows (5) cost about 20 us of transfers, an eighth of what I said, and PE hid it; the figures of the Trainium skill, held against their own full rate, didn't carry that rival either.

**The range** ended at 4700 us because I took the two optimistic ends as separate cases: cheap stores with the coupled dense part, or the floor with 7 us stores. Cheap stores (80 us less) together with the dense part at 1678 us (62 us less) bring 4830 us to 4688 us; no case of mine held both. That this lies so near the measured time is luck in part: the entry with the queries was 24 us longer, the rest of the building, the closing and the small remainders shorter by nearly as much.

## What to carry to other kernels

Of a DMA that an engine issues itself, cost the issue by what is still under way in that queue when it comes, not by its size: spaced, a 2 MB store in 4096 pieces cost ACT 0.37 us; behind one that wasn't through, 6 to 16 us. When two resources come out within a few per cent of each other, the coupling was small here where the engine in order was the later one and the transfers ran ahead in a ring (57 us in 1678, half of it at the start), and larger where neither had slack (8%); test with both sides lightened, since lightening either alone shows nothing. A layout cost that an experiment doesn't find may only be hidden: ask again in a kernel where the transfers come last, and read the time of the queue's packets beside the time of the kernel. When a wait is moved in a queue, look at what stands behind its new place.

## What the runs showed of the hardware that I had not expected

- The issue of a store held ACT while the store before wasn't through: 5.7 to 14.9 us for a pair, 8.8 to 15.7 us at a distance of 10 to 12 us with the transfers full, and 0.37 to 0.72 us at 10 to 22 us with a DMA share of 0.79. How much of the store before has to be gone, no run shows.
- The time of a busy PE group went with its columns: 16 records of 128x256 took 3.62 us where 16 of 128x384 took 5.32 us, 0.68 of it for two thirds of the columns. The durations of single records (0.379 and 0.486 us) overlap and hide that.
- PE pays for a wait twice. The same 16 records took 6.30 us behind a wait of 10.4 us, at a granted clock of 0.57, and 3.62 us without one, at 1.00; over the thin kernel's dense part the granted clock was 0.94 with PE busy for 86%, and 0.99 in the changed kernel with 97%.
- 2 MB stored in pieces of 512 bytes beside a full gather took 33 us to land, 64 GB/s, and 40 us in the two kernels with U loads issued beside it; the last of the twelve is what the next part had to wait for.
